# HGRN2 decay spans from one running sum of the log gates: seven products per tile replaced by differences on VectorE

## What is computed

```python
def _hgrn2_recurrence(q, k, v, log_f):
    # S_t = diag(f_t) S_(t-1) + k_t v_t^T with k_t = 1 - f_t,  o_t = S_t^T q_t  (chunkwise)
    bc = jnp.cumsum(_to_chunks(log_f), axis=-2)
    def step(S, inp):
        q_n, k_n, v_n, b_n = inp
        diff = b_n[..., :, None, :] - b_n[..., None, :, :]
        dec = jnp.where(causal3, jnp.exp(jnp.where(causal3, diff, 0.0)), 0.0)
        a = jnp.einsum('bhid,bhjd,bhijd->bhij', q_n, k_n, dec)
        o = jnp.einsum('bhid,bhde->bhie', q_n * jnp.exp(b_n), S) + jnp.einsum('bhij,bhje->bhie', a, v_n)
        b_last = b_n[..., -1:, :]
        S = S * jnp.exp(b_last)[..., 0, :, None] + jnp.einsum('bhjd,bhje->bhde', k_n * jnp.exp(b_last - b_n), v_n)
        return S, o
```

## Time and profile before

| | us |
|---|---|
| median of 3 runs | 1835.48 |
| lowest and highest run | 1833.47, 1836.23 |
| the profiled execution: span from first to last instruction | 1839.9 |
| PE busy | 1606.1 (87%) |
| VectorE (DVE) busy | 998.2 (54%) |
| ScalarE (ACT) busy | 452.3 (25%) |
| GpSimd (POOL) busy | 314.6 (17%) |
| DMA | 471.32 MB, mean 256 GB/s |

### The profile page before, as it was taken

One profiled execution on the slowest core, in us unless ns is written; L12 is line 12 of the kernel. 1 busy time (PEld: TensorE's weight loads), 2 busy tenths in 40 slices (PEclk: granted clock), 3 DMA queues, 4 the chain that ended last, 5 costly groups with the idle time before them and its releaser, 6 DMA issues.

```text
span 1839.9 us, 19400 instructions
## 1 busy us (share of the span) xinstructions
PE 1606.1 (87%) x7684; PEld 1073.9 (58%) x7684; DVE 998.2 (54%) x1847; ACT 452.3 (25%) x1009; POOL 314.6 (17%) x269
## 2 busy tenths in 40 slices
PE   7999989999898888989568756668999999899998
PEld 6857656765745554446224322227997486489963
DVE  2433325331767786458997666562665414356654
ACT  1142143330225543123333222221000013210001
POOL 0000000000113544333446444510000000000000
PEclk9989999999998998999779898898999999999999
DMA  6445221126798999999999999992543443154433
GB/s 237 167 153 183 92 92 46 46 85 245 306 424 355 401 419 420 406 413 419 417 420 421 422 421 422 422 404 98 217 180 141 183 160 137 46 210 180 175 146 114
DMA packets 55193, 471.32 MB, mean 256 GB/s; under 512 B 6593, under 2 KB 7745, under 8 KB 10433
## 3 DMA queue, kind: packets, MB, share of 16 engines
q0 software_dynamic: 36864, 268.45, 35.3%
q1 hardware_dynamic: 18240, 201.66, 29.0%
HBM read 469.04 MB, written 1.05 MB: 255 GB/s over the span
## 4 chain that ended last, share of the span: by engine, by line
PE 64%; DMA 16%; DVE 12%; ACT 4%; issue 3%; POOL 1%; SPq 0%; DVEq 0%; ACTq 0%; POOLq 0%
DMA main<-in_expert_uv,main 13%; PE ps L2431 13%; PE ps L489 7%; PE ps L445 6%; PE ps L1014 6%; PE ps L2588 5%; PE ps L415 5%; PE ps L1252 4%; DVE main L942 3%; PE ps L2358 3%; PE ps L1486 3%; PE ps L2377 2%; PE ps L485 2%; DMA panels<-in_wall 2%; PE ps L2354 2%
## 5 line engine op out<-in xcount | busy, mean ns | idle before, releaser
L1014 PE MATMUL ps<-main 128*128 128x512 f32 x660 | 336.8, 659 | 118.0 <-ACT main L989 117.8
L924 POOL DMA_INDIRECT main<-in_expert_uv,main x208 | 253.5, 1219 | 390.5 <-PE ps L1014 197.4
L1014 PEld LDWEIGHTS ps<-main 128*128 128x128 f32 x660 | 133.0, 211 | 300.4 <-ACT main L989 157.4
L942 DVE SCALAR_TENSOR_TENSOR main<-main 128x1024 f32<-128x1024 f32 x208 | 249.9, 1223 | 101.4 <-DMA main<-in_expert_uv,main 100.4
L977 ACT ACTIVATE main<-main 128x2 f32<-128x2 f32 x128 | 26.0, 203 | 360.3 <-DVE main L942 291.2
L445 PE MATMUL ps<-panels,xT 128*128 128x512 f32 x256 | 112.5, 592 | 0.0
L2431 PE MATMUL ps<-main 128*128 128x128 f32 x912 | 104.9, 275 | 0.0
L2431 PEld LDWEIGHTS ps<-main 128*128 128x128 f32 x912 | 103.4, 192 | 0.0
L1014 PE MATMUL ps<-panels,main 128*128 128x512 f32 x152 | 74.7, 634 | 23.3 <-ACT main L989 23.3
L1252 PEld LDWEIGHTS ps<-main 128*128 128x128 f32 x704 | 82.1, 192 | 10.9 <-issue 9.2
L415 PE MATMUL ps<-xT,panels 128*128 128x256 f32 x384 | 84.9, 385 | 1.3 <-PEq L582 1.3
(11 more groups left out here) (319 smaller groups left out, 2327.1 us busy)
## 6 DMA issues: line engine op xcount, KB each, us to landing
panels<-in_wall SPq DMA_DIRECT2D x87, 2048.0 KB
main<-in_rows SPq DMA_DIRECT2D x14, 512.0 KB, 7.8
main<-in_expert_uv,main POOLq DMA_INDIRECT x208, 16.4
main<-in_sub_keys SPq DMA_DIRECT2D x2, 1024.0 KB, 12.6
main<-in_wall SPq DMA_DIRECT2D x1, 2048.0 KB, 12.5
mats<-in_mats SPq DMA_DIRECT2D x1, 1088.0 KB, 5.5
x<-in_x SPq DMA_DIRECT2D x2, 512.0 KB, 4.0
main<-in_pool_w SPq DMA_DIRECT2D x1, 1024.0 KB
```

What stands on the lines that cost most here:

```text
L924: pool.indirect_dma_start(out=self.bufs[self.buf_of[r]], out_offset=None, in_=self.c.dram["expert_uv"], in_offset=bass.IndirectOffsetOnAxi ...
L942: dve.scalar_tensor_tensor(out=u, in0=u, scalar=1.0, in1=self.c.row(m, H2), op0=ALU.mult, op1=ALU.mult, accum_out=self.dots_at[:, m, q:q + ...
L1014: mm = pe.matmul(self.c.ps[:, b, :], self.diags[self.of_pe(r) % DIAG_RING], v[:, half * HALF:(half + 1) * HALF], start=(q == 1), stop=(q = ...
```

## The change

- The seven `span` matrices and their products go. Instead PE makes one product `sum` for each tile: `log_f` times `upto`, the running sum of the log gates. ACT copies it over `log_f` (`t.sums`).
- In each level DVE makes the spans as two differences of 128x512: the running sum less that of the last token of the left half, and the reverse for the left half. ACT takes Exp of them in place, from SBUF to SBUF.
- `to_end`, its Exp and its product with k move from the end of tile 0's levels to the head, before the levels. `e_b` of tile 1 is Exp of the running sum, without a product of its own.
- In the hand-written order the differences of level l + 1 are made right behind `both` of level l, and the rest of the level follows. Some stops of `hgrn1` move by a few rows.

```diff
 MATS = (["ident", "upto", "after", "ones"]
-        + [f"span{l}" for l in range(LEVELS)] + [f"level{l}" for l in range(LEVELS)])
+        + [f"level{l}" for l in range(LEVELS)])
 MAT = {n: i for i, n in enumerate(MATS)}
 
 ROWS = ["b_low0", "b_low1", "norm2", "final_norm", "pool_scale", "ln_mix_g0", "ln_mix_b0",
...
@@ -1044,9 +1044,8 @@
 
 def hgrn_units(m):
 
-    units = {"k_t": ["k_t", "same"], "ends": ["e_b"] if m else ["to_end"], "o": ["o"] if m else ["o", "s"]}
-    for l in range(LEVELS):
-        units.update({f"span{l}": [f"span{l}"], f"a{l}": [f"a{l}"]})
+    units = {"k_t": ["k_t", "same", "sum"] if m else ["k_t", "same", "to_end", "sum"], "o": ["o"] if m else ["o", "s"]}
+    units.update({f"a{l}": [f"a{l}"] for l in range(LEVELS)})
     return units
 
 
@@ -1360,11 +1359,21 @@
             slots = [slot(n) for n in range(6)]
         self.both, self.a_qk, self.log_f, self.k_t, self.kT, self.span = slots
         self.lb, self.lb1 = c.part(1, I_B), c.part(1, Q_B)
+        self.sums = self.log_f
         self.e_b, self.q_dec, self.k_dec, self.o, self.squared = (
-            self.span, self.both, self.kT, self.log_f, self.a_qk)
+            self.span, self.both, self.k_t, self.log_f, self.a_qk)
         self.S = slot(STATE_B)
         self.stat = c.small[:, 304 + 32 * m:336 + 32 * m]
         self.un = lambda name: f"hgrn{m}.{name}"
+
+
+def hgrn_steps():
+
+    steps = ["span0", "both0"]
+    for l in range(LEVELS):
+        steps += ([f"span{l + 1}"] if l + 1 < LEVELS else []) + [f"a{l}", f"pick{l}"]
+        steps += [f"both{l + 1}"] if l + 1 < LEVELS else []
+    return steps
 
 
 def hgrn_scalar(c, m, act):
@@ -1385,25 +1394,21 @@
     act.activation(t.log_f, t.f, ACT.Ln).then_inc(c.up("log_f"), 1)
     act.wait_ge(*un.full(name("k_t")))
     act.activation(t.kT, un.view(name("k_t")), ACT.Copy).then_inc(un.freed(name("k_t")), 1)
+    if m == 0:
+        act.wait_ge(*un.full(name("to_end")))
+        act.activation(t.span, un.view(name("to_end")), ACT.Exp).then_inc(un.freed(name("to_end")), 1)
+    act.wait_ge(*un.full(name("sum")))
+    act.activation(t.sums, un.view(name("sum")), ACT.Copy).then_inc(un.freed(name("sum")), 1)
     yield "k_t"
-    for l in range(LEVELS):
-        yield f"span{l}"
-        act.wait_ge(*un.full(name(f"span{l}")))
-        if l:
-
-            act.wait_ge(*c.at("both", m, 2 * l))
-        act.activation(t.span, un.view(name(f"span{l}")), ACT.Exp).then_inc(un.freed(name(f"span{l}")), 1)
-        yield f"both{l}"
-        yield f"a{l}"
-        yield f"pick{l}"
+    for stop in hgrn_steps():
+        if stop.startswith("span"):
+            l = int(stop[4:])
+            act.wait_ge(*c.at("spans_made", m, l + 1))
+            act.activation(t.span, t.span, ACT.Exp).then_inc(c.up("decayed"), 1)
+        yield stop
     if m:
-        act.wait_ge(*un.full(name("e_b")))
         act.wait_ge(*c.at("both", m, 2 * LEVELS))
-        act.activation(t.e_b, un.view(name("e_b")), ACT.Exp).then_inc(un.freed(name("e_b")), 1)
-    else:
-        act.wait_ge(*un.full(name("to_end")))
-        act.wait_ge(*c.at("both", m, 2 * LEVELS))
-        act.activation(t.k_dec, un.view(name("to_end")), ACT.Exp).then_inc(un.freed(name("to_end")), 1)
+        act.activation(t.e_b, t.sums, ACT.Exp).then_inc(c.up("e_b"), 1)
     yield "ends"
     yield "o"
     act.wait_ge(*un.full(name("o")))
@@ -1439,33 +1444,42 @@
     dve.wait_ge(*un.full(name("same")))
     dve.tensor_tensor(t.a_qk, un.view(name("same")), spread(c.mat("ident"), HEADS),
                       ALU.mult).then_inc(un.freed(name("same")), 1)
-    yield "k_t"
-    for l in range(LEVELS):
-        halves = lambda x: x.rearrange("p h (b s t) -> p h b s t", s=2, t=1 << l)
-        yield f"span{l}"
-        dve.wait_ge(*un.read_out(name(f"span{l}")))
-        if l == 0:
-            dve.wait_ge(*un.read_out(name("k_t")))
-        for side, x in ((1, t.qT), (0, t.kT)):
-            dve.tensor_tensor(halves(t.both)[:, :, :, side, :], halves(x)[:, :, :, side, :],
-                              halves(t.span)[:, :, :, side, :], ALU.mult).then_inc(c.up("both"), 1)
-        yield f"both{l}"
-        yield f"a{l}"
-        dve.wait_ge(*un.full(name(f"a{l}")))
-        if l == 0:
-            dve.wait_ge(*un.read_out(name("same")))
-        else:
-            dve.wait_ge(*un.read_out(name(f"a{l - 1}")))
-        dve.copy_predicated(out=t.a_qk, mask=spread(c.masks[:, l, :], HEADS),
-                            data=un.view(name(f"a{l}"))).then_inc(un.freed(name(f"a{l}")), 1)
-        yield f"pick{l}"
-    if m:
-        dve.wait_ge(*un.read_out(name("e_b")))
-        dve.tensor_tensor(t.q_dec, t.qT, t.e_b, ALU.mult).then_inc(c.up("q_dec_b"), 1)
-    else:
+    if m == 0:
         dve.wait_ge(*un.read_out(name("to_end")))
         dve.wait_ge(*c.at("k_b", m))
-        dve.tensor_tensor(t.k_dec, t.k_dec, t.k_t, ALU.mult).then_inc(c.up("k_dec_b"), 1)
+        dve.wait_ge(*un.full(name("k_t")))
+        dve.tensor_tensor(t.k_dec, t.k_t, t.span, ALU.mult).then_inc(c.up("k_dec_b"), 1)
+    yield "k_t"
+    halves = lambda x, l: x.rearrange("p h (b s t) -> p (h b) s t", s=2, t=1 << l)
+    for stop in hgrn_steps():
+        l = int(stop[-1])
+        if stop.startswith("span"):
+            if l == 0:
+                dve.wait_ge(*un.read_out(name("sum")))
+                if m == 0:
+                    dve.wait_ge(*c.at("k_dec_b"))
+            else:
+                dve.wait_ge(*c.at("both", m, 2 * l))
+            sums, span = halves(t.sums, l), halves(t.span, l)
+            middle = sums[:, :, 0, (1 << l) - 1:1 << l].broadcast_to([P, HEADS * P >> (l + 1), 1 << l])
+            dve.tensor_tensor(span[:, :, 1, :], sums[:, :, 1, :], middle, ALU.subtract)
+            dve.tensor_tensor(span[:, :, 0, :], middle, sums[:, :, 0, :], ALU.subtract).then_inc(c.up("spans_made"), 1)
+        elif stop.startswith("both"):
+            dve.wait_ge(*c.at("decayed", m, l + 1))
+            if l == 0:
+                dve.wait_ge(*un.read_out(name("k_t")))
+            for side, x in ((1, t.qT), (0, t.kT)):
+                dve.tensor_tensor(halves(t.both, l)[:, :, side, :], halves(x, l)[:, :, side, :],
+                                  halves(t.span, l)[:, :, side, :], ALU.mult).then_inc(c.up("both"), 1)
+        elif stop.startswith("pick"):
+            dve.wait_ge(*un.full(name(f"a{l}")))
+            dve.wait_ge(*un.read_out(name(f"a{l - 1}" if l else "same")))
+            dve.copy_predicated(out=t.a_qk, mask=spread(c.masks[:, l, :], HEADS),
+                                data=un.view(name(f"a{l}"))).then_inc(un.freed(name(f"a{l}")), 1)
+        yield stop
+    if m:
+        dve.wait_ge(*c.at("e_b"))
+        dve.tensor_tensor(t.q_dec, t.qT, t.e_b, ALU.mult).then_inc(c.up("q_dec_b"), 1)
     yield "ends"
     yield "o"
     yield "S"
@@ -1496,25 +1510,21 @@
     for b in (0, 2):
         pe.wait_ge(c.bank_read[b].sem, c.uses_at[f"b_q.{m}"][b])
     heads("same", lambda h: t.kT[:, h, :], lambda h: t.qT[:, h, :])
-    yield "k_t"
     pe.wait_ge(*c.at("log_f", m))
-    for l in range(LEVELS):
-
-        heads(f"span{l}", lambda h: t.log_f[:, h, :], lambda h: c.mat(f"span{l}"))
-        yield f"span{l}"
-        yield f"both{l}"
-        pe.wait_ge(*c.at("both", m, 2 * (l + 1)))
-        heads(f"a{l}", lambda h: t.both[:, h, :], lambda h: t.both[:, h, :])
-        yield f"a{l}"
-        yield f"pick{l}"
-    if m:
-        heads("e_b", lambda h: t.log_f[:, h, :], lambda h: c.mat("upto"))
-    else:
+    if m == 0:
         pe.wait_ge(*un.emptied(name("to_end")))
         for b in range(2):
             mm = pe.matmul(un.view(name("to_end"), 2)[:, b, :], c.mat("after"),
                            flat(t.log_f)[:, b * HALF:(b + 1) * HALF], start=True, stop=True)
         mm.then_inc(un.filled(), 1)
+    heads("sum", lambda h: t.log_f[:, h, :], lambda h: c.mat("upto"))
+    yield "k_t"
+    for stop in hgrn_steps():
+        if stop.startswith("a"):
+            l = int(stop[1:])
+            pe.wait_ge(*c.at("both", m, 2 * (l + 1)))
+            heads(f"a{l}", lambda h: t.both[:, h, :], lambda h: t.both[:, h, :])
+        yield stop
     yield "ends"
     pe.wait_ge(*un.read_out(name(f"a{LEVELS - 1}")))
     if m:
@@ -1920,29 +1930,29 @@
     part("read0", 13)
     part("hgrn0", "k_t")
     part("delta1", "norm")
-    part("hgrn0", "span0", "both0")
+    part("hgrn0", "span0", "both0", "span1")
     part("delta1", "turn")
     part("hgrn0", "a0", "pick0")
     part("beside0", 14)
     part("read0", 14)
     part("delta1", "decay")
-    part("hgrn0", "span1", "both1")
+    part("hgrn0", "both1", "span2")
     part("delta1", "kk")
     part("hgrn0", "a1", "pick1")
     part("delta1", "P0", "XY0")
-    part("hgrn0", "span2", "both2")
+    part("hgrn0", "both2", "span3")
     part("beside0", 15)
     part("read0", 15)
     part("delta1", "P1")
     part("hgrn0", "a2", "pick2")
...
@@ -2005,37 +2015,33 @@
     part("read1", 5)
     part("tile0", "top4", "best4", "name4")
```

(28 more changed lines are left out.)

10 lines of the change are left out of this document (5 added, 5 removed).

## The result

| | us |
|---|---|
| the changed kernel, median of 20 runs | 1839.91 (1834.40 to 1846.32) |
| the kernel before, median of 20 runs beside them | 1836.22 (1831.09 to 1840.03) |
| ratio | 1.0022, 95% interval 1.0014 to 1.0031 |
| the profiled execution of the changed kernel: its time, its span | 1837.62, 1835.8 |

What follows compares the result with a forecast made beforehand. PE was taken to bound hgrn0, the gathers hgrn1. Terms -6.0 + 0.9 + 3.7 = -1.4 us took the profiled 1839.9 to 1838.5 and the runs from 1835.48 to 1834.0 us; range 1829.0 to 1840.0.

Steps and rivals of the forecast that it cites:

- Head of hgrn0: Start of hgrn0: the longer chain through ACT and DVE makes a0 and the panel half behind it 8.1 us later.
- Clock: Head of hgrn0: new idle stretches may leave PE at the lower clock; +0.9 us, between 0 and 1.8.
- Given back: hgrn0 behind its head: 12.4 us of PE slots and 1.7 us of stalls go, leaving -6.0 us after the head.
- a sign of being wrong: End of hgrn0: branch products expected at about 405 to 406 us; starting before 403 or after 410 refutes the forecast.
- rival 3: hgrn0 does not shorten, as new stalls take the spans' slots; gain 0, hgrn1's head cost stays: 1839.2 us, chance 0.15.
- Head of hgrn1: Start of hgrn1: row 18's sum comes 4.7 us later and delays a gather; +3.7 us, between 0 and 4.7.
- the 1 us of cover: Head of hgrn1: queued transfers were to hide 1 us of the late gather's 4.7 us delay.
- Rest of hgrn1: hgrn1 behind its head: PE sheds 10.7 us, DVE gains 8.5, its Exp waits mostly go; worth 0 while gathers bound.
- a subtraction, 0.6 us: DVE in both tiles: each added subtraction was priced at about 0.6 us.
- rival 2: DVE starves the gathers through all of hgrn1, adding 8.5 us: +7.1, 1842.6 us; decided by DVE reaching 95%; chance 0.12.
- Skill against rows: ACT table switches in both heads: 1.28 us by the rows; the page's added 1.38 drain would give 1836.6 us.

Runs made afterwards that it cites:

- run 3: Changed kernel with ACT's copy of delta1's turned k put ahead of the Exp of span1 in hgrn0's head; ratio 0.9994 to the kernel before.
- run 8: hgrn1 as before; hgrn0 changed, its head reordered: norm products first, turned k's copy before every Exp, a panel half ahead of a0; 1824.75 us against 1840.65, ratio 0.9911.
- run 6: Changed kernel with hgrn1's stops in their old places, plus hgrn1's subtractions from level 1 on made twice; ratio 1.0028, against 1.0005 without the doubling.
- run 4: Changed kernel with the experts' row groups put back between the stops of hgrn1's head; ratio 1.0011 to the kernel before.
- run 11: Second trace of the unchanged kernel before: branch products 150.8 us and hgrn1's turned k 327.3 us after hgrn0's turned k.
- runs 7 and 8: 7: changed kernel, delta1's norm products ahead of to_end and sum, turned k's copy ahead of span1's Exp; 0.9968. 8: filled hgrn0 head, hgrn1 as before; 0.9911.

## Why the prediction was wrong

- **Head of hgrn0, +8.1.** This step failed. The panel half started 14.3 us later from the mark. Of that, the norm products are 6.7 late (I had 5.8) and the turned k 6.8 (5.7), so the chain through ACT was right to about 1 us. The missing piece is that a0 waited, after `both0` was ready, another 3.5 us for delta1's copy behind Exp of span1. I had followed the units of PE and the order of ACT, but not which unit shares a pair with which reader. Run 3 takes it away. Of the 6.2 us beyond the forecast 1.0 is the chain's (`both0` done 26.5 us from the mark, 25.5 forecast), 3.5 this wait and 1.7 a0's slower clock.
- **Clock, +0.9 (0 to 1.8).** a0 took 3.75 instead of 2.05 us and the panel half 8.12 instead of 7.03: 2.8 us, beyond my upper end: the granted clock was 0.50 from 288.8 to 294.0 us, and 1.00 over the same work before (278 to 290 us). The idle time before a0 alone doesn't explain it: in run 3 that is 1.67 instead of 4.69 us, and both are as slow. In run 8 a0 behind a panel half took 1.95 us and the half itself 7.96, so about 1 us of loss is left there.
- **Given back, 12.4 of slots and 1.7 of stalls.** Right: 13.7 us between the panel half and the branch products once its slower clock is set aside.
- Together hgrn0 stands at 14.3 + 1.1 - 13.7 = +1.7 us against the first trace of before and at -0.5 against the second, not at **-6.0** + 0.9 = -5.1. Counted from the mark, the branch products lie at 262.28 + 150.31 = 412.6 on the scale of before, later than the 410 that I had named as a sign of being wrong. That is rival 3's outcome (the measured 1839.9 us is near its 1839.2), though not by its reason: no new stalls took the slots, the head ate them.
- **Head of hgrn1, +3.7 (0 to 4.7).** The place and the mechanism held: from the mark the first dot is 3.75 us late (I had 3.9), the sum of row 18 starts 4.5 late (4.7). The size was short. That sum took 5.40 us instead of 3.60 (granted clock 0.68 over it, 1.00 over the same sum in the kernel before), so the gather went out 5.7 us late; and the 1 us of cover that I granted was none. Cost 5.4 to 6.0 us by the windows, 5.5 by the run with hgrn1 alone (interval 3 to 8).
- **Rest of hgrn1, 0; a subtraction, 0.6 us; rival 2.** Right: 0.69 us each, 0.6 apart, and no second hole. DVE's waits for Exp there fell from 16.4 to 1.1 us, and DVE was busy 80.2 of 90 us (592 to 682), 89% where the rival named 95%. That rival was nearer than it looked (run 6).
- **Skill against rows.** The rows stood: 1.28 us for a load and the Exp at 598.07 right behind the load at 596.78 (run 4). The drain of 1.38 us that the Trainium skill, ScalarE: Activation LUTs, section What ACT_TABLE_LOAD costs, adds is not there. The price by the page was also summed short: two drains of 1.38 are 2.8 us, not 2.6.

The forecast of 1834.0 lies 2.2 us under before's median beside it; measured is 3.7 over. The two heads that I had under-priced, 5 to 7 us in hgrn0 and about 2 in hgrn1, make 7 to 9 us of that difference of 5.9. So the parts come to 1 to 3 us too much, within the intervals of the ratios (about 2 us each); they do not prove the sum.

**What stays open.** Ahead of hgrn1 the transfers dip a second time in every kernel, by different amounts, and hgrn1's turned k lies 309 to 328 us behind hgrn0's. By run 11 the stretch behind the branch products goes with the chip and not with hgrn0's arithmetic; why, no run shows. Which chip the first trace of before and that of the changed kernel came from isn't on record, so their difference of 6.6 us in that stretch is not put down to the change. Single traces scatter by some 4 us against their medians. Open too is why run 3 is at least 2 us and runs 7 and 8 some 2.5 us faster than branch products and lost transfers account for; that is about the width of the intervals. And why PE's clock stays low in one head and not in another was not found.
